# RWKV norm and output projection of a two-layer diffusion backbone: norm among the scan steps, projection among the norm, no barriers between

## The reference

```python
y = ys[0] + ys[1]                                   # forward and backward scan
mu = jnp.mean(y, -1, keepdims=True)                 # over the 64 channels of a head
var = jnp.mean(jnp.square(y - mu), -1, keepdims=True)
y = ((y - mu) * lax.rsqrt(var + GN_EPS)).reshape(B, T, RW)
y = y * lp['ln_g'] + lp['ln_b'] + (bonuses[0] + bonuses[1]).reshape(B, T, RW)
g = jax.nn.sigmoid(hf @ lp['g1']) @ lp['g2']
o_rw = y * g
...
out = jnp.concatenate([o_att, o_rw], -1) @ lp['w_o']    # 640x1024 by 1024x1024
x = x + gate * rmsnorm(out)                             # then norm for the channel part
```

## Time and profile before

| | |
|---|---|
| median of 3 runs | 2768.53 us (2764.76 to 2773.94) |
| profiled execution | 2758.32 us, its span 2756.5 us |
| busy TensorE, VectorE, ScalarE, GpSimd | 2566.4, 1398.8, 1099.9, 174.2 us |
| mean granted clock of TensorE | 0.976 of 2.4 GHz |
| chain that ended last | TensorE 84%, VectorE 9%, ScalarE 2%, "issue" 2%, DMA 1% |
| layer 0, last scan iteration to the first tile of the projection | about 630 to 694 us of the span |
| the same in layer 1 | about 1797 to 1861 us |

### The profile page before, as it was taken

One profiled execution on the slowest core, in us unless ns is written; L12 is line 12 of the kernel. 1 busy time (PEld: TensorE's weight loads), 2 busy tenths in 40 slices (PEclk: granted clock), 3 DMA queues, 4 the chain that ended last, 5 costly groups with the idle time before them and its releaser, 6 DMA issues.

```text
span 2756.5 us, 64283 instructions
## 1 busy us (share of the span) xinstructions
PE 2566.4 (93%) x28404; PEld 2278.1 (83%) x28404; DVE 1398.8 (51%) x2490; ACT 1099.9 (40%) x2054; POOL 174.2 (6%) x179
## 2 busy tenths in 40 slices
PE   6998799997999999989987999979999999999996
PEld 4996588786798989969965878857899999999995
DVE  2337455555433333362375545564555555555566
ACT  3226444444421212242255444443444444444452
POOL 0002101110000000010010111100100000000011
PEclk8999899998999999989999999989999999999998
DMA  6223123200122222222200330001655555555572
GB/s 270 77 77 125 42 85 125 94 34 5 62 77 72 75 75 77 77 73 69 77 18 1 125 124 4 4 5 62 258 208 184 207 213 188 203 208 211 180 256 86
DMA packets 82685, 304.33 MB, mean 110 GB/s; under 512 B 9376, under 2 KB 9504, under 8 KB 82272
## 3 DMA queue, kind: packets, MB, share of 16 engines
q1 hardware_dynamic: 71072, 257.93, 26.1%
q0 software_dynamic: 11328, 42.21, 4.2%
HBM read 273.11 MB, written 27.00 MB: 109 GB/s over the span
## 4 chain that ended last, share of the span: by engine, by line
PE 84%; DVE 9%; ACT 2%; issue 2%; DMA 1%; POOL 0%; SPq 0%; DVEq 0%; ACTq 0%; POOLq 0%
PE ps L448 19%; PE ps L449 19%; PE ps L450 19%; PE ps L1199 6%; PE ps L1207 3%; PE ps L806 2%; PE ps L461 2%; PE ps L911 2%; PE ps L954 1%; PE ps L1110 1%; PE ps L970 1%; DMA ring<-in_blocks 1%; PE ps L814 1%; DVE arena L2383 1%; DVE arena L2382 1%
## 5 line engine op out<-in xcount | busy, mean ns | idle before, releaser
L2190 DVE TENSOR_TENSOR ring_lo<-ring,w_ffn 128x1024 fp32r<-128x1024 f32 x264 | 322.4, 1225 | 214.5 <-ACT w_ffn L1660 208.7
L448 PE MATMUL ps<-hg_hi,w_ffn 128*128 128x256 f32 x1408 | 401.8, 285 | 0.9 <-DVE hg_lo L2782 0.9
L449 PE MATMUL ps<-hg_lo,w_ffn 128*128 128x256 f32 x1408 | 397.5, 282 | 0.0
L450 PE MATMUL ps<-hg_hi,ring_lo 128*128 128x256 f32 x1408 | 397.0, 282 | 0.0
L1660 ACT ACTIVATE w_ffn<-ring 128x1024 fp32r<-128x1024 f32 x264 | 278.1, 1057 | 197.8 <-PE ps L450 197.3
L448 PEld LDWEIGHTS ps<-hg_hi,w_ffn 128*128 128x128 f32 x1408 | 266.8, 189 | 2.5 <-DVE hg_lo L2782 1.1
L449 PEld LDWEIGHTS ps<-hg_lo,w_ffn 128*128 128x128 f32 x1408 | 265.8, 189 | 1.2
L450 PEld LDWEIGHTS ps<-hg_hi,ring_lo 128*128 128x128 f32 x1408 | 266.4, 189 | 0.0
L450 PE MATMUL ps<-hT_ffn_hi,ring_lo 128*128 128x320 f32 x704 | 215.6, 306 | 0.0
L448 PE MATMUL ps<-hT_hi,w_proj 128*128 128x320 f32 x672 | 206.3, 307 | 6.8 <-DVE hT_lo L2196 6.8
L449 PE MATMUL ps<-hT_lo,w_proj 128*128 128x320 f32 x672 | 208.6, 310 | 0.0
(11 more groups left out here) (382 smaller groups left out, 5216.1 us busy)
## 6 DMA issues: line engine op xcount, KB each, us to landing
ring<-in_blocks SPq DMA_DIRECT2D x484, 512.0 KB, 3.3
h_rows<-arena POOLq DMA_DIRECT2D x16, 512.0 KB, 10.1
arena<-h_rows POOLq DMA_DIRECT2D x7, 1024.0 KB, 9.4
y_rows<-arena POOLq DMA_DIRECT2D x7, 1024.0 KB, 6.6
x<-in_x_all SPq DMA_DIRECT2D x1, 2560.0 KB, 13.4
h_plain<-arena POOLq DMA_DIRECT2D x1, 2560.0 KB, 17.3
out_y_all<-x POOLq DMA_DIRECT2D x5, 512.0 KB, 3.6
w<-in_low POOLq DMA_DIRECT2D x2, 768.0 KB, 6.5
```

The source lines that it names most:

```text
L448: nc.tensor.matmul(dst, w_hi, m_hi, start=start, stop=False)
L449: nc.tensor.matmul(dst, w_hi, m_lo, start=False, stop=False)
L450: return nc.tensor.matmul(dst, w_lo, m_hi, start=False, stop=stop)
L2190: V.tensor_tensor(ring_lo[:, n % RING, :], ring[:, n % RING, :], high[:, n % high.shape[1], :], ALU.subtract).then_inc(*E.sig("w_lo"))
```

## The change

The two barriers are gone: each engine's list runs on, with waits for single results. What moves:

- The `head_mean` products and bonuses of pairs 0 to 2 and the bonus of pair 3 go among the seven scan steps of the ninth iteration (`gn_early`, on TensorE behind each `scan_step`, on VectorE behind each update); the writes of `bon_sel` go to that iteration's start. Only pair 3's mean must wait for the last y.
- The splits of weight block 0 and of `oT` group 0 go to the start of the ninth iteration; those of blocks 1 to 4 among the norm, those of 5 to 7 behind the pairs that free their space.
- Tiles 0 and 1 of the projection run block by block inside `gn_phase` (`wo_first`): blocks 0 to 3, which come from attention, stand among the norm, 4 and 5 follow pairs 0 and 1, 6 and 7 come last, behind both row vectors. `wo_phase` starts with tile 2.
- Norm spreads all use PSUM pair 3 and gates pair 2, so each waits for VectorE's step on the pair before.
- The 16 diagonals on ScalarE go ahead of the spreads. `sq4`, `spr`, `stat_rows` and `bon_sel` lie elsewhere in the arena.
- GpSimd signals `kr_prod` (the r * k product is in place) and waits for the states alone (`so_ev`) before it stores them.

The diff, cut to its core (the removed bodies of `gn_phase` and `wo_phase` stand in the listing above):

```diff
-cursor[0] = MIX_END
-sq4 = take(4 * T, c=4, t=T)
-spr = take(2 * T, b=2, t=T)
-stat_rows = take(T)
-bon_sel = take(NPAIR * P, c=NPAIR, t=P)
+sq4 = arena[:, K_TOK_AT:K_TOK_AT + 4 * T].rearrange("p (c t) -> p c t", c=4)
+spr = arena[:, AMV_AT:AMV_AT + 2 * T].rearrange("p (b t) -> p b t", b=2)
+stat_rows = kds
+bon_sel = ra[:, 1, :, :].rearrange("p j t -> p (j t)")[:, 0:NPAIR * P].rearrange("p (c t) -> p c t", c=NPAIR)
...
                 scan_step(b, s)
+                if a is None:
+                    gn_early(l, s)
...
-        next_phase()
+    def gn_mean(l, c, dst):
+        mm640(nc, dst, C("head_mean"), oT[:, 4 + c, :], True, True).then_inc(sem["gn_mean_mm"], 1)
+    def gn_bonus(l, c, dst):
+        pe.wait_ge(sem["gn_sel"], l * NPAIR + c + 1)
+        pe.wait_ge(sem["kr_prod"], l * NPAIR + c + 1)
+        mm640(nc, dst, bon_sel[:, c, :], rkv[:, 4 + c, :], True, True).then_inc(sem["gn_bon_mm"], 1)
+    def gn_early(l, s):
+        if s in (2, 3):
+            gn_mean(l, s - 2, s - 2)
+        if s == 5:
+            pe.wait_ge(sem["gn_cent"], l * NPAIR + 1)
+            gn_mean(l, 2, 0)
+        if s == 1:
+            gn_bonus(l, 0, 3)
+        if s in (4, 6):
+            c = s // 2 - 1
+            pe.wait_ge(sem["gn_bon"], l * NPAIR + c)
+            gn_bonus(l, c, 3)
+        if s == 7:
+            pe.wait_ge(sem["gn_cent"], l * NPAIR + 2)
+            gn_bonus(l, 3, 1)
+    def wo_part(l, i, h, fc):
+        half, tok = slice(h * 512, (h + 1) * 512), slice(i * P, (i + 1) * P)
+        mm = mm_split(nc, pair(i % 2)[:, half], oT_hi[:, fc, tok], oT_lo[:, fc, tok], w_wo[:, fc, half],
+                      ring_lo[:, (WO_AT[l] + fc) % RING, half], fc == 0, fc == WO_B - 1)
+        if fc == WO_B - 1 and (i < NT - 1 or h == 0):
+            mm.then_inc(sem["wo_mm"], 1)
+        return mm
+    def wo_first(l, i, fc):
+        if i == 0:
+            pe.wait_ge(sem["x_lo"], X_FFN[l] - WO_B + fc + 1)
+            pe.wait_ge(sem["w_lo"], split[0] + fc + 1)
+        for h in range(2):
+            wo_part(l, i, h, fc)
+    def gn_gate(l, c):
+        if c == 0:
+            pe.wait_ge(sem["sums_ev"], 2 * l + 2)
+        else:
+            pe.wait_ge(sem["gn_used"], 8 * l + 2 * c)
+        mm640(nc, 2, w2[:, 2, c * P:(c + 1) * P], zlow[:, 2, :], True, True).then_inc(sem["gn_mm"], 1)
+    def gn_norm(l, c):
+        pe.wait_ge(sem["spread_ev"], 8 * l + 4 + c + 1)
+        if c == 0:
+            pe.wait_ge(sem["gn_rs"], l + 1)
+        else:
+            pe.wait_ge(sem["gn_used"], 8 * l + 2 * c - 1)
+        spread(pair640(3), spr[:, c % 2, :]).then_inc(sem["gn_mm"], 1)
     def gn_phase(l):
...
         pe.wait_ge(sem["gn_cent"], l * NPAIR + 3)
+        wo_first(l, 0, 0)
+        pe.wait_ge(sem["y_ev"], UNITS * (l + 1))
+        pe.wait_ge(sem["gn_bon"], l * NPAIR + 3)
+        gn_mean(l, 3, 3)
+        wo_first(l, 0, 1)
+        wo_first(l, 0, 2)
         head_sums(2 * l + 1, 2, sq4, "gn_sq")
...
+        wo_first(l, 0, 3)
         pe.wait_ge(sem["gn_cent"], NPAIR * (l + 1))
         turn_sums(2 * l + 1, 3, stat_rows)
...
-        next_phase()
+        gn_gate(l, 0)
+        pe.wait_ge(sem["gn_bon"], NPAIR * (l + 1))
+        for fc in range(3):
+            wo_first(l, 1, fc)
+        gn_norm(l, 0)
+        wo_first(l, 1, 3)
+        gn_norm(l, 1)
+        gn_gate(l, 1)
+        gn_norm(l, 2)
+        gn_gate(l, 2)
+        wo_first(l, 0, 4)
+        gn_norm(l, 3)
+        wo_first(l, 1, 4)
+        gn_gate(l, 3)
+        wo_first(l, 0, 5)
+        wo_first(l, 1, 5)
+        pe.wait_ge(sem["gn_used"], 8 * (l + 1))
+        mix_rowvec(l, 0)
+        mix_rowvec(l, 1)
+        for fc in (6, 7):
+            wo_first(l, 0, fc)
+            wo_first(l, 1, fc)
...
         a, b = unit_at(l, it), unit_at(l, it - 1)
+        if a is None:
+            act.wait_ge(sem["kr_prod"], NPAIR * (l + 1))
+            act.wait_ge(sem["rw_ops"], 4 * UNITS * (l + 1))
+            act.wait_ge(sem["mv_mm"], b + 1)
+            wo_weight(l, 0)
+            wo_high(l, 0)
         if b is not None:
             act.wait_ge(sem["wu_mm"], 2 * b + 1)
...
+    def gn_square(l, c):
+        act.wait_ge(sem["gn_cent"], l * NPAIR + c + 1)
+        A(sq4[:, c, :], oT[:, 4 + c, :], ACT.Square).then_inc(*E.sig("gn_sq"))
     def gn_phase(l):
...
+        wo_weight(l, 1)
+        wo_high(l, 1)
+        wo_high(l, 2)
+        act.wait_ge(sem["mt_ev"], 2 * UNITS * (l + 1))
+        wo_high(l, 3)
+        gn_square(l, 0)
+        act.wait_ge(sem["gn_bon_mm"], l * NPAIR + 1)
+        wo_weight(l, 2)
+        gn_square(l, 1)
+        gn_square(l, 2)
+        act.wait_ge(sem["gn_bon_mm"], NPAIR * (l + 1))
+        wo_weight(l, 3)
+        wo_weight(l, 4)
+        gn_square(l, 3)
         rows_out(2 * l + 1, 2, stat_rows)
...
         act.wait_ge(sem["mix_gate"], l + 1)
         for n in range(16):
             A(mix_diags[:, n, :], ident, ACT.Copy, scale=gpost[:, 0, n % 8, n // 8:n // 8 + 1]).then_inc(*E.sig("rowvec_diag"))
-        next_phase()
+        act.wait_ge(sem["gn_rs"], l + 1)
+        spread(0, 0, spr[:, 0, :]).then_inc(*E.sig("spread_ev"))
+        spread(0, 1, spr[:, 1, :]).then_inc(*E.sig("spread_ev"))
+        act.wait_ge(sem["gn_mm"], 8 * l + 2)
+        spread(0, 2, spr[:, 0, :]).then_inc(*E.sig("spread_ev"))
+        act.wait_ge(sem["gn_used"], 8 * l + 2)
+        wo_high(l, 4)
+        act.wait_ge(sem["gn_mm"], 8 * l + 3)
+        spread(0, 3, spr[:, 1, :]).then_inc(*E.sig("spread_ev"))
+        act.wait_ge(sem["gn_used"], 8 * l + 4)
+        wo_weight(l, 5)
+        wo_high(l, 5)
+        act.wait_ge(sem["gn_used"], 8 * l + 6)
+        wo_high(l, 6)
+        act.wait_ge(sem["gn_used"], 8 * l + 8)
+        wo_weight(l, 6)
+        wo_weight(l, 7)
+        wo_high(l, 7)
...
+        if a is None:
+            dve.wait_ge(sem["tk_tr"], 3 * (b + 1))
+            for c in range(NPAIR):
+                V.tensor_scalar(bon_sel[:, c, :], C("head_mean"), PR(l, "r_k", c), float(HD), ALU.mult, ALU.mult).then_inc(*E.sig("gn_sel"))
+            wo_low(l, 0)
...
+            if a is None:
+                gn_early(l, s)
...
+    def gn_early(l, s):
+        if s in (3, 4):
+            gn_center(l, s - 3, s - 3)
+        if s == 6:
+            gn_center(l, 2, 0)
+        if s in (2, 5, 7):
+            gn_bonus(l, s // 2 - 1, 3)
+        if s == 8:
+            gn_bonus(l, 3, 1)
+            wo_low(l, 1)
+            wo_low(l, 2)
+    def gn_pair(l, c):
+        y = oT[:, 4 + c, :]
+        at = 8 * l + 2 * c
+        dve.wait_ge(sem["gn_mm"], at + (2 if c == 0 else 1))
+        V.scalar_tensor_tensor(y, y, PR(l, "ln_g", c), pair640(3), ALU.mult, ALU.mult).then_inc(*E.sig("gn_used"))
+        dve.wait_ge(*E.own_last())
+        V.scalar_tensor_tensor(y, y, PR(l, "ln_b", c), rkv[:, 8 + c, :], ALU.add, ALU.add).then_inc(*E.sig("dve_step"))
+        dve.wait_ge(*E.own_last())
+        dve.wait_ge(sem["gn_mm"], at + 2)
+        V.tensor_tensor(y, y, pair640(2), ALU.mult).then_inc(*E.sig("gn_used"))
     def gn_phase(l):
+        wo_low(l, 3)
+        gn_center(l, 3, 3)
         post_scale(l, 0)
         pre_scale(l, 1)
         post_scale(l, 1)
...
+        wo_weight(l, 4)
         rsqrt_sums(2 * l + 1, 3, 1.0 / HD, GN_EPS, "gn_rs")
...
-        next_phase()
+        gn_pair(l, 0)
+        gn_pair(l, 1)
+        x_lo(oT_lo[:, 4, :], oT[:, 4, :], oT_hi[:, 4, :])
+        gn_pair(l, 2)
+        wo_low(l, 5)
+        gn_pair(l, 3)
+        wo_low(l, 6)
+        wo_low(l, 7)
...
-        next_phase()
...
-        next_phase()
+        pool.wait_ge(sem["so_ev"], UNITS * (l + 1))
```

More of the change, by code:

```diff
@@ L295, in build @@
         btok = bb[:, :, :, 1, :]
+        K_TOK_AT = cursor[0]
         ktok = take(T, i=NT, h=2, t=CH)
@@ L1334, in gn_phase @@
-                next_phase()
-            def wo_phase(l):
-                first = used[0]
-                mix_rowvec(l, 0)
-                for i in range(NT):
-                    if i >= 2:
-                        pe.wait_ge(sem["post_tmp"], post_before(2 * l) + 2 * (i - 1))
-                    tok = slice(i * P, (i + 1) * P)
-                    def part(h, fc):
-                        half = slice(h * 512, (h + 1) * 512)
-                        return mm_split(nc, pair(i % 2)[:, half], oT_hi[:, fc, tok], oT_lo[:, fc, tok], w_wo[:, fc, half],
-                                        ring_lo[:, (first + fc) % RING, half], fc == 0, fc == WO_B - 1)
-                    if i == 0:
-                        for fc in range(WO_B):
-                            pe.wait_ge(sem["w_lo"], split[0] + fc + 1)
-                            for h in range(2):
-                                mm = part(h, fc)
-                                if fc == WO_B - 1:
-                                    mm.then_inc(sem["wo_mm"], 1)
-                            if fc == 0:
-                                mix_rowvec(l, 1)
-                        continue
+                gn_gate(l, 0)
@@ L1358, in wo_phase @@
```

(14 more changed lines are left out.)

91 lines of the change are left out of this document (26 added, 65 removed).

## The result

The changed kernel takes 2735.1 us (median of four runs, 2732.9 to 2736.0), the kernel before beside it 2767.3: a ratio of 0.988, 95% interval 0.986 to 0.990. Forecast were 2738 us and a ratio of 0.989. The profiled execution of the changed kernel took 2735.5 us.

The account below looks back on a forecast made before the run. TensorE, busy 93% of the span, was taken as the bound, so only its idle or slow-clock time could shrink. Tile 2 starting 15.1 us sooner per layer, 30.2 in all, gave a 2738 us median, range 2731 to 2746.

Parts of the forecast that it names:

- Ahead of the scan steps: Before the first scan step: added ScalarE copies (1.6 us) and VectorE work (2.7 us) fit in existing gaps.
- Scan steps: Last scan iteration: each step with a 640-column product takes 1.49 us, 0.29 of it for switching tiling; 10.6 us in all.
- The y products: Behind the scan steps: dense TensorE work keeps 2.4 GHz, so they take 2.8 us instead of 4.9.
- Wait for y: Ahead of the fourth mean: TensorE idles 1.2 us because the y add queues behind VectorE's bonus and two splits.
- Norm: Norm phase: first spread hidden with 0.7 us to spare; gates 1 and 2 each wait 0.9 us for VectorE.
- Tile 2: Start of tile 2: waits for tile 0's PSUM pair, with 0.7 to 1.0 us showing.
- Barriers: At the two removed barriers: their cost is inside the idle time already counted, with no separate price.
- The sum: Both layers: tile 2 starts 15.1 us sooner per layer, 30.2 us in all.
- The cross-check by gains: Per layer: 12.1 us idleness and 6.3 slow clock gained, 3.8 new idleness and 2.0 switching returned, leaving 12.6.
- The clock did not fall again: Rival, in the stage: 1.2 GHz spells cost 6.3 us per layer as before, median 2751; chance 0.15.
- The gaps did not close by themselves: Rival, in the stage: switching nearly free and VectorE keeps up, 3.8 + 2 us more per layer, median 2727; chance 0.1.
- The signs: In the trace: clock 1.00, steps every 1.5 us, the predicted waits, tile 2 at 52.7 us, 33.3 us behind it unchanged.

Follow-up runs that it names:

- the 64x64 form: Changed kernel with the seven norm products among the scan steps written as 64x64 products of the two heads; 2725.9 us, ratio 0.988 to before.
- the dummy products: Kernel before with one unread 512-column product behind each scan step of the ninth iteration, nothing moved; 2765.4 us, ratio 1.000 to before.
- the block moves: Changed kernel with blocks 2 and 3 of tile 1 each moved one place later, ahead of the second gate; 2728.0 us, ratio 0.987 to before.
- the three edits: Changed kernel with block 2's split behind the y add, two tile 1 blocks moved later and early norm products in 64x64 shape; 2725.4 us, again 2724.6.
- the kernel with the norm behind y: Changed kernel with the norm products of three pairs taken from the scan steps and put behind the y products; 2745.8 us, ratio 0.995 to before.

## Why the prediction was right, point by point

Counted from the first scan step (637.50 in the working, 636.85 in the profile of the changed kernel), the walk along TensorE stands against the trace like this:

| event | predicted | measured |
|---|---|---|
| y products start | 10.6 | 10.9 |
| y products end | 13.4 | 13.8 |
| fourth mean | 15.9 | 16.4 |
| head sums | 19.9 | 20.4 |
| first norm product | 28.3 | 29.0 |
| gate 1 | 31.7 | 32.4 |
| gate 2 | 34.4 | 35.0 |
| row vectors | 42.7 | 43.4 |
| tile 2 | 52.7 | 53.1 |

*What bounds the kernel* held: no large product changed, tile 2 takes 11.10 us as tile 1 did, and both layers gave the same.

*Ahead of the scan steps.* Covered as said: the idle time ahead of the first step is 1.59 us in both traces.

*Scan steps.* 1.54 us instead of 1.49, the largest miss between two lines of this table: 0.3 us over seven steps. The row that I took the price from, a product one iteration earlier, is in 64*128 form and not in 128*128 form as I read it; the way from the product to the next 64x64 one costs the same (1.28 and 1.27 us), the way from the scan step to the product 0.27 us instead of 0.21. That the surplus is the change of layout was an argument; the 64x64 form shows it.

*The y products.* 2.87 us for 2.8. The cause, the clock, was read off one longer matmul; the dummy products show it.

*Wait for y.* 1.00 us idle, released by the y add, for 1.2. The queue ahead of it is the cause, as the edit that shortens it shows.

*Norm.* The first spread is hidden, as predicted, for TensorE was not idle ahead of it. It needs the first spread alone, and the pair of them ends at 665.58; where the block moves asked for it sooner, it came 0.8 us sooner (28.2 for 29.0 us), so some 0.8 us were to spare for 0.7. Gates 1 and 2 wait 0.81 and 0.67 us for 0.9 each, by VectorE's three steps per pair, as said.

*Tile 2.* It waits 0.40 us, for 0.7 to 1.0. Tile 0's PSUM pair is freed by L2692 as predicted. Here two misses cancel: tile 0's last matmul ends 51.2 us after the first scan step (the next starts at 688.01) where the walk had 50.3 (687.8 less 637.5), and the shorter wait gives half of these 0.9 us back. That the end agrees to 0.4 us is in part luck.

*Barriers.* In before TensorE's idle time at them is 1.17 and 3.44 us. Put back into the new order they cost more, 3.9 (with the two splits moved) and 4.1 us a layer, 8.0 of the 14.8 that the whole change gains. Had I been asked for the second one alone I would have been too low by 2.4 us. The prediction did not lean on such a price, because it walked the order of every queue up to tile 2.

*The sum.* Predicted 15.1 us a layer, measured 14.8, so 29.5 in all. Medians taken side by side gave 32.1 and 33.6; the two profiles of each kernel differ by 26.9 in the mean. The stages are the firm number, and the others lie about it by the scatter outside the stage. The cross-check by gains gave 12.6 and was too low in both its terms. Idle time in the stage fell from 12.2 us to 3.0, by 9.2 where it had 12.1 - 3.8 = 8.3. Busy time fell from 55.6 us to 50.2, by 5.5 where it had 6.3 - 2.0 = 4.3. How much of the 1.2 us between is the tails in the busy time, which the prediction named, and how much is spells at the low clock priced too low, is not separated.

*The rivals.* The clock did not fall again. The gaps did not close by themselves; they do with the three edits, for 8.5 us of the 11.6 that this rival would have given. The changed order does remove waiting. No stretch of low clock appeared in the stage.

*The signs.* What was to show in the stage did. Two signs against the prediction showed behind it. Tiles 2 to 4 of layer 0 take 33.7 us (689.98 to 723.67) and not 33.3. That is not the change, for before has both paces: its matmuls of 512 columns follow each other every 0.231 us in layer 0 (705.40 to 711.88, 28 of them) and every 0.233 in layer 1 (1871.87 to 1875.37, 15 of them), the latter as here. And in the dense phase of layer 0 the clock dips for some 3 us in both profiles of the changed kernel. TensorE's row in the changed kernel, and the same matmul in before:

```profile
735.83 0.47 PE L450 MATMUL ps<-hT_lo,w_first 128*128 128x320 f32 x1
```

```profile
750.43 0.31 PE L449 MATMUL ps<-hT_lo,w_first 128*128 128x320 f32 x1
```

It costs 1.4 us there (733.76 to 746.29 against 748.77 to 759.92). Nine of the thirteen profiles have it; those of before, of the block moves and of the 64x64 form do not. Whether the change makes it likelier is not shown.

## What to carry to other kernels

A chain of short, dependent steps is a place to put independent work of the stage behind it, and the two halves of such a change support each other: products that stood serially in the norm kept the clock up in the scan, and blocks of the projection had nothing left to wait for. Walk the queue of every engine to the first point that is unchanged, and price each wait by what stands ahead of the awaited instruction in its engine's queue; that gave the stage here to 0.9 us in 51 ahead of its last wait, and to 0.4 in 53 with it. Judge gains of a few us by the length of the stage in a trace, for the whole program's time moves by more than that with the granted clock elsewhere.

## What the runs showed of the hardware that was not expected

- Equal code fell to half clock in one execution and not in the next: 11 us at 0.53 against 1.00, behind the same idle time of 1.23 us. In the runs of one kernel the time goes with the mean clock: the 64x64 form ran 2724.4, 2725.4 and 2726.5 us at 0.982, 0.981 and 0.981, and 2734.0 at 0.976.
- A change between 64x64 and 128x128 products costs 0.35 us for there and back, with no idle time shown by the trace: it lies within the busy time of the rows.
- The clock fell during the scan steps with no idle time over 0.67 us between their matmuls. In the kernel with the norm behind y it had fallen by the second step in layer 0 (0.48 us at 637.96) and by the fourth in layer 1 (1802.20), in before by the sixth (641.48), with the same matmuls on TensorE.
- Equal matmuls of 512 columns followed each other every 0.231 us in one layer and every 0.233 in the other, in one execution of before and at a granted clock of 1.00. Over tiles 2 to 4 that is 0.3 to 0.4 us.
